# Two transformer blocks on one core: block 2's scores as two fp32r products on high and low halves, entry and end reordered

## The reference

```
def windowed_gqa(q, k, v, sink):
    qb = (q * (HEAD_DIM ** -0.5)).reshape(B, nb, BLOCK, N_KV_HEADS, Q_GROUP, HEAD_DIM)
    kb = band_blocks(k.reshape(B, S, N_KV_HEADS, HEAD_DIM), nb)
    ...
    scores = jnp.einsum("bnqhgd,bnkhd->bnhgqk", qb, kb).astype(jnp.float32)
    ...
    scores = scores - slopes * absdist.astype(jnp.float32)
    ...
    m = jnp.maximum(jnp.max(scores, axis=-1, keepdims=True), sink_l)
    p = jnp.exp(scores - m)
    denom = jnp.sum(p, axis=-1, keepdims=True) + jnp.exp(sink_l - m)
    p = (p / denom).astype(v.dtype)
    out = jnp.einsum("bnhgqk,bnkhd->bnqhgd", p, vb)
```

## Time and profile before

| what | value |
|---|---|
| time, median of 3 runs | 690.18 us (689.23 to 691.2) |
| the profiled execution's own time | 689.03 us |
| its span, first to last instruction | 687.2 us |
| TensorE busy, share of the span | 640.4 us, 93% |
| VectorE busy | 351.2 us, 51% |
| ScalarE busy | 290.0 us, 42% |
| GpSimd busy | 51.7 us, 8% |
| chain that ended last: TensorE, transfers, VectorE, ScalarE | 76%, 11%, 6%, 4% |

### The profile page before, as it was taken

How to read it: one execution, slowest core, us unless ns; L and a number is a source line. 1 busy time by engine, 2 the same in 40 slices (tenths; PEclk the granted TensorE clock), 3 DMA queues, 4 the chain that set the end, 5 groups by cost and what they waited for, 6 DMA issues and landing times.

```text
span 687.2 us, 10211 instructions
## 1 busy us (share of the span) xinstructions
PE 640.4 (93%) x4037; PEld 483.7 (70%) x4037; DVE 351.2 (51%) x678; ACT 290.0 (42%) x552; POOL 51.7 (8%) x76
## 2 busy tenths in 40 slices
PE   8999899999999776879899999999999999999995
PEld 5979888842543320424399999998788888888884
DVE  4687664731031020110187766657856666666665
ACT  5855562421011010100182755563665555544554
POOL 3100101100010000000049000000000000000001
PEclk9999999999999997799999999999999999999999
DMA  8956338999999999999997333345535555554101
GB/s 344 419 194 260 116 138 331 403 372 426 427 374 425 420 422 421 422 420 421 422 421 280 123 124 123 123 167 187 185 137 188 189 195 202 198 193 184 62 1 61
DMA packets 26286, 180.73 MB, mean 263 GB/s; under 512 B 3184, under 2 KB 3312, under 8 KB 5120
## 3 DMA queue, kind: packets, MB, share of 16 engines
q1 hardware_dynamic: 25488, 177.89, 65.4%
q10 hardware_dynamic: 752, 2.21, 0.8%
HBM read 179.04 MB, written 1.05 MB: 262 GB/s over the span
## 4 chain that ended last, share of the span: by engine, by line
PE 76%; DMA 11%; DVE 6%; ACT 4%; issue 2%; POOLq 0%; SPq 0%; POOL 0%; ACTq 0%; DVEq 0%
PE ps L1567 73%; DMA ring<-stream_dram 11%; PE ps L1570 3%; DVE ring_r L406 1%; ACT single L399 1%; DVE work L1502 1%; ACT work L850 1%; DVE work L1505 1%; ACT work L757 0%; DVE h L1555 0%; ACT turned L855 0%; ACT work_r L846 0%; DVE work L1388 0%; DVE single L1399 0%; ACT work L764 0%
## 5 line engine op out<-in xcount | busy, mean ns | idle before, releaser
L1567 PE MATMUL ps<-turned,single 128*128 128x256 f32 (+2 forms) x944 | 231.1, 326 | 1.6 <-ACT work L627 0.8
L1567 PE MATMUL ps<-turned,ring_r 128*128 128x256 f32 (+1 forms) x648 | 179.9, 281 | 0.0
L1567 PEld LDWEIGHTS ps<-turned,single 128*128 128x128 f32 x944 | 156.3, 189 | 18.4 <-issue 2.0
L406 DVE TENSOR_TENSOR ring_r<-ring,single 128x1024 fp32r<-128x1024 f32 (+1 forms) x132 | 160.8, 1240 | 14.7 <-ACT single L399 14.7
L399 ACT ACTIVATE single<-ring 128x1024 fp32r<-128x1024 f32 (+1 forms) x132 | 133.8, 1047 | 0.0
L1567 PEld LDWEIGHTS ps<-turned,ring_r 128*128 128x128 f32 x648 | 121.2, 189 | 0.4
L1567 PE MATMUL ps<-ring,work 128*32 128x512 f32 (+2 forms) x462 | 69.8, 612 | 14.7 <-DMA ring<-stream_dram 12.6
L1567 PEld LDWEIGHTS ps<-single 128*128 128x128 f32 x257 | 40.7, 199 | 34.8 <-issue 22.4
L1567 PE MATMUL ps<-work 128*128 128x128 f32 (+5 forms) x310 | 60.5, 378 | 2.6 <-DVE work L1046 1.8
L1567 PE MATMUL ps<-single,turned 128*128 128x512 f32 (+3 forms) x208 | 59.7, 367 | 1.9 <-DVE turned L1187 1.5
L1567 PE MATMUL ps<-single 128*128 128x512 f32 (+1 forms) x257 | 58.0, 367 | 2.9 <-DVE single L1399 1.9
(11 more groups left out here) (254 smaller groups left out, 697.4 us busy)
## 6 DMA issues: line engine op xcount, KB each, us to landing
ring<-stream_dram SPq DMA_DIRECT2D x145, 1024.0 KB, 12.0
work<-stream_dram SPq DMA_DIRECT2D x12, 1024.0 KB, 12.3
turned_w<-stream_dram SPq DMA_DIRECT2D x4, 1024.0 KB, 14.1
extra<-stream_dram SPq DMA_DIRECT2D x2, 1024.0 KB, 9.4
ring<-stream_dram SPq DMA_DIRECT2D x2, 832.0 KB, 7.2
h<-x_dram SPq DMA_DIRECT2D x2, 512.0 KB, 4.5
gain<-gains_dram ACTq DMA_DIRECT2D x2, 512.0 KB, 8.5
yields<-stream_dram SPq DMA_DIRECT2D x1, 1024.0 KB, 12.5
```

The costliest lines, as they stand in the source:

```text
L406: dve.tensor_tensor(ring_r[:, place, a], ring[:, place, a], w_hi[k % HIGHS][:, a].bitcast(F32), ALU.subtract).then_inc(s["wlo_done"], 1)
L1567: return pe.matmul(o, lhsT, rhs, start=start, stop=stop, **kw)
```

## The change

Block 2's scores: `q2_split` and `k2_split` are laid over `extra`, whose tiles have been read by then. For each query head `q2_split` holds the high half in the head's own 64 rows and the low half in the other 64 rows. For each key head `k2_split` holds the high half of K in both halves of the rows, and, for each place of the query head, the low half in 64 rows and zeros elsewhere (GpSimd clears these instead of `k2T`). The first product of a unit then gives high x high and low x high at once, the second high x low. ScalarE makes the high halves (`q2_high`, `k2_high`) between its weight splits, VectorE the low ones (`q2_low`, `k2_low`), three pairs ahead of the loop and three inside it, in units 3, 4 and 6. The two turns of K on TensorE and ScalarE's copies of them are gone.

The entry: TensorE, and with it the first transposes, waits for `cst`, `meta` and the first half of `h` alone; `vec` is issued by ScalarE as its second load; three idle products stand instead of four, and two instead of four later. The end: the last squares stand ahead of the second result; ScalarE itself issues the store of the third piece; SP's last store waits only for its own piece.

```
+        q2_split = halved(extra_r[:, 0, :], HEADS, TOK)
+        k2_split = halved(extra_r[:, 1, :], 6, TOK)
...
+        def q2_high(act, c):
+            act.wait_ge(s["q2_sb"], c + 1)
+            for hd in (2 * c, 2 * c + 1):
+                rows = q2_rows(hd, 0)
+                last = act.activation(q2_split[rows, hd, :], q2T[rows, c, :], ACT.Copy)
+            last.then_inc(s["qk_high"], 1)
...
+        def q2_low(dve, c):
+            dve.wait_ge(s["qk_high"], c + 1)
...
+                last = dve.tensor_tensor(q2_split[q2_rows(hd, 1), hd, :], q2T[rows, c, :], q2_split[rows, hd, :].bitcast(F32),
+                                         ALU.subtract)
...
+        def k2_low(dve, kv):
+            dve.wait_ge(s["zpad_done"], 3)
+            dve.wait_ge(s["qk_high"], CT + 2 * kv + 1)
...
-            sp.dma_start(vec[:, 0:V_RB], small[:, 0:V_RB]).then_inc(const_in, 16)
...
             act.dma_start(meta_raw, meta).then_inc(x_in, 16)
+            act.dma_start(vec[:, 0:V_RB], small[:, 0:V_RB]).then_inc(const_in, 16)
             act.dma_start(pos_i[:], positions).then_inc(const_in, 16)
...
             result(0, 0)
+            last_squares(1, 1)
             result(0, 1)
-            last_squares(1, 1)
             result(1, 0)
+            act.wait_ge(s["y_done"], NT + 1)
+            act.dma_start(out[P:TOK, 0:512], xn2[:, 1, column_half(0)]).then_inc(out_st, 16)
...
-            idle_products(ps[:, 7, 0:ZA], zt[:, 0, 0:P], zt[:, 0, :], 4)
-            pe.wait_ge(const_in, 48)
-            pe.wait_ge(x_in, 32)
+            idle_products(ps[:, 7, 0:ZA], zt[:, 0, 0:P], zt[:, 0, :], 3)
+            pe.wait_ge(x_in, 48)
...
-            idle_products(ps[:, 0, 0:ZA], zt[:, 0, 0:P], zt[:, 0, :], 4)
+            idle_products(ps[:, 0, 0:ZA], zt[:, 0, 0:P], zt[:, 0, :], 2)
...
-            mm(ps[0:HD, 1, 0:TOK], ident[:, HD:P], k2T[:, 3, :], True, True)
-            mm(ps[HD:P, 1, 0:TOK], ident[:, 0:HD], k2T[:, 0, :], True, True).then_inc(s["k2_ps"], 1)
...
             def scores2(u):
                 hd, i = u // 2, u % 2
-                if u == 2:
-                    pe.wait_ge(s["k2_sb"], 2)
+                kv = hd // 4
+                if u % 8 == 0:
+                    pe.wait_ge(s["qk_high"], CT + 2 * kv + 2)
+                    pe.wait_ge(s["qk_low"], 5 if kv else 3)
+                elif u == 12:
+                    pe.wait_ge(s["qk_low"], CT + 2)
                 if u >= 2:
                     pe.wait_ge(s["nm2_done"], u - 1)
-                mm(ps[:, 2 + u % 2, 0:TOK], q2T[:, hd // 2, i * P:(i + 1) * P], k2T[:, 2 * (hd // 4) + hd % 2, :],
-                   True, True).then_inc(s["s2_ps"], 1)
+                q = q2_split[:, hd, i * P:(i + 1) * P]
+                mm(ps[:, 2 + u % 2, 0:TOK], q, k2_split[:, kv, :], True, False)
+                mm(ps[:, 2 + u % 2, 0:TOK], q, k2_split[:, 2 + 2 * kv + hd % 2, :], False, True).then_inc(s["s2_ps"], 1)
```

More of the change, by code:

```diff
@@ L311, in two_blocks @@
         full = [sem(f"slot_full{i}") for i in range(SLOTS)]
-        extra_full = [sem(f"extra_full{i}") for i in range(EXTRA)]
         full2 = [sem(f"slot2_full{i}") for i in range(SLOTS)]
@@ L468, in attention2_low, with q2_rows, k2_high @@
                               ).then_inc(s["o2_low"], 1)
+        def q2_rows(hd, low):
+            return slice(HD, P) if hd % 2 != low else slice(0, HD)
+        def q2_high(act, c):
[6 more added lines that the diff above has]
+            dve.wait_ge(s["qk_high"], c + 1)
+            for hd in (2 * c, 2 * c + 1):
+                rows = q2_rows(hd, 0)
+                last = dve.tensor_tensor(q2_split[q2_rows(hd, 1), hd, :], q2T[rows, c, :], q2_split[rows, hd, :].bitcast(F32),
+                                         ALU.subtract)
+            last.then_inc(s["qk_low"], 1)
+        def k2_high(act, kv):
+            act.wait_ge(s["q2_sb"], CT + 1)
+            rows = slice(kv * HD, (kv + 1) * HD)
+            for other in (kv, 1 - kv):
+                act.activation(k2_split[other * HD:(other + 1) * HD, kv, :], k2T[rows, :], ACT.Copy).then_inc(s["qk_high"], 1)
+        def k2_low(dve, kv):
+            dve.wait_ge(s["zpad_done"], 3)
+            dve.wait_ge(s["qk_high"], CT + 2 * kv + 1)
+            rows = slice(kv * HD, (kv + 1) * HD)
+            for odd in (kv, 1 - kv):
+                to = slice(odd * HD, (odd + 1) * HD)
+                last = dve.tensor_tensor(k2_split[to, 2 + 2 * kv + odd, :], k2T[rows, :], k2_split[rows, kv, :].bitcast(F32),
+                                         ALU.subtract)
+            last.then_inc(s["qk_low"], 1)
         def gate_out(dve, m):
@@ L570, in _ @@
                              ).then_inc(full2[n % SLOTS], 16)
-            for i in range(NT):
-                for n in range(2):
-                    sp.wait_ge(s["y_done"], n + 1 if i == 0 else 2 * NT)
-                    sp.dma_start(out[i * P:(i + 1) * P, n * 512:(n + 1) * 512], xn2[:, i, n * 512:(n + 1) * 512]
-                                 ).then_inc(out_st, 16)
+            for n in range(2):
+                sp.wait_ge(s["y_done"], n + 1)
+                sp.dma_start(out[0:P, n * 512:(n + 1) * 512], xn2[:, 0, n * 512:(n + 1) * 512]).then_inc(out_st, 16)
+            sp.wait_ge(s["y_left"], 1)
+            sp.dma_start(out[P:TOK, 512:D], xn2[:, 1, 512:D]).then_inc(out_st, 16)
             sp.wait_ge(out_st, 16 * 2 * NT)
@@ L805, in _ @@
             split_high(act, SPLIT1 + 3)
+            q2_high(act, 0)
             split_high(act, SPLIT1 + 4)
+            q2_high(act, 1)
+            q2_high(act, 2)
             split_high(act, SPLIT1 + 5)
-            act.wait_ge(s["zpad_done"], 3)
-            act.wait_ge(s["k2_ps"], 2)
-            for c in range(2):
-                rows = slice((1 - c) * HD, (2 - c) * HD)
-                last = act.activation(k2T[rows, c + 1, :], ps[rows, 1, 0:TOK], ACT.Copy)
-            last.then_inc(s["k2_sb"], 1)
+            q2_high(act, 3)
+            k2_high(act, 0)
+            k2_high(act, 1)
             def values_out():
@@ L1454, in _ @@
                     split_low(dve, SPLIT1 + 3 + c // 2)
+                else:
+                    q2_low(dve, c // 2)
             dve.wait_ge(s["k2_ps"], 1)
-            dve.wait_ge(s["zpad_done"], 3)
-            for c in range(2):
-                rows = slice(c * HD, (c + 1) * HD)
-                last = dve.tensor_tensor(k2T[rows, 3 * c, :], ps[rows, 0, 0:TOK], row2[rows, :], ALU.mult)
-            last.then_inc(s["k2_sb"], 1)
+            dve.tensor_tensor(k2T, ps[:, 0, 0:TOK], row2, ALU.mult).then_inc(s["q2_sb"], 1)
+            k2_low(dve, 0)
             split_low(dve, SPLIT1 + 5)
```

36 lines of the change are left out of this document (21 added, 15 removed).

## The result

The changed kernel takes 683.67 us (median of 4 runs, 683.35 to 684.21) against 689.7 (688.82 to 691.2): a ratio of 0.9911, with a 95% interval of 0.9898 to 0.9925. The runs of before are the three that stood ahead of the prediction, with a median of 690.18, and one more of 688.82. The forecast was 684.6. The profiled execution took 683.71 us with a span of 681.9, 5.3 less than the span of before.

What follows compares the result with a forecast made beforehand. TensorE was taken to carry 76% of the chain of waits. Entry 1.65, block 2 3.0 and end 0.9 sum to 5.55 us: 684.6 us from the median 690.18, 683.5 from the profiled execution; range 682.4 to 687.0.

Steps and rivals of the forecast that it cites:

- The entry (1.65): Start of the kernel: earlier transposes and fewer idle products were to gain 1.65 us, bounds 0.9 and 2.0.
- So it does not wait: Entry: sixteen transposes lie ahead of the one needing `h`'s second half, due at 6.84 us, so no wait there.
- TensorE gets to its higher clock as early as before: Entry: condition under which the removed idle products cost nothing else, TensorE working without a pause up to there.
- rival *slower: Entry: TensorE pauses for a late load, clock stays at 1.2 GHz into the first products; 692 us and more; chance 0.04.
- Passing the expert stage: Expert stage, between entry and block 2: its beginning and end move with TensorE, so the whole 1.65 us passes.
- My rival in which the stage swallows the entry: Expert stage: if transfers set its start, the entry's 1.65 us is lost; 686.2 us; chance 0.13.
- Block 2's start (0.7): First scores of block 2: 0.88 us cheaper on TensorE, of which 0.7 counts, with a wait at the second turn.
- the first rival: Block 2's start: K's two low subtractions each wait behind a GpSimd operation; start worth 0.2, time 685.1 us; chance 0.17.
- The loop (2.3): Block 2's loop: two cheaper score products per unit, 12 units left at 0.19 us each, 2.3 us.
- the margin of 0.3: Block 2's loop, two units: with a pair VectorE needs 3.7 us to the next softmax row; TensorE comes after 4.0.
- the third rival: Block 2's loop: VectorE bounds it, or the new pair is not cheaper; loop gives 0.3, time 686.6 us; chance 0.12.
- The end (0.9): Last row: squares one scaling earlier, 0.47 us, and last store from ScalarE, 0.43; 0.9 taken, bounds 0.47 and 0.95.

## Why the prediction was right, step by step

- **The entry (1.65).** Right in size: 1.43 in the two profiles, 1.6 in the mean of the traces. Two steps failed singly. "So it does not wait" for `h`'s second half: it did in that execution, because a landing of 5.2 us is one of 4.8 to 6.1; TensorE also came for it earlier than forecast, with the transposes starting at 5.69 us and not 6.2. And that TensorE gets to its higher clock as early as before: in two executions of six it did not, and their marks are some 1.6 us behind the mean of the other four (14.15). That is the lower clock of my rival *slower*, but without the pause that the rival names, and I had given it 15 us of work at half rate. The rows show that it ended with the transposes or within the next idle product; so it takes most of the entry's gain in such an execution, and no more.
- **Passing the expert stage.** Right: whole, with -0.8 to +1.2 us on top, in which no run shows a gain or a loss by the change. Without +0.66 of that the profiled pair would differ by 4.7 and not 5.3. My rival in which the stage swallows the entry falls: at 150 us the shift was 1.47, at 342 us 2.09.
- **Block 2's start (0.7).** 0.67 and a wait at the second turn, as forecast, but by two errors that cancel. K's low pair took 1.73 us where I had put 0.85 + 0.4, since GpSimd stood beside both halves: the mechanism of the first rival, with the wait at the first score that I had named as a sign of being wrong. In turn GpSimd was done before the weight split behind it, which took 2.36 us and not the 3.02 of the earlier trace rows, and it ended when I had said. The rival's price, 0.5 of the start, was therefore not paid; without GpSimd the start is 0.46 better.
- **The loop (2.3).** Mechanism right, size off: 1.95. The units are 3.76 us (3.77 forecast), so the new pair is as much cheaper as the gate chunk's products said. The term mis-sized is the margin of 0.3: from the gate chunk's end (394.57) to the turn (398.52) VectorE and ScalarE needed 3.95 us, where I had 3.7, and TensorE came after 3.79, where I had 4.0. A margin of -0.16, in each of the two units: a part of the third rival (VectorE bounds the loop), 0.4 us of the 2.0 that I had given it. Moving the pairs gave it back (0.41).
- **The end (0.9).** 0.64. The squares gave their 0.47 (0.45 at the last scaling). The term mis-sized is the store: 0.43 forecast, about 0.2 measured, since the issue came 0.37 sooner but that store landed 2.4 us after it, and not 2.2. On SP the end is worth the same, so ScalarE's queue gained nothing; what helped was that SP's stores no longer wait for all the pieces (the last one issued 0.89 us behind the start of the last scaling, 1.12 before).
- **The sum.** 5.55 forecast; 5.3 in the profiles, 6.0 in the medians. The median fell 0.9 us below the forecast. Half of that is the base: the median of before was 690.18 with three runs and is 689.7 with four. The other half is 6.0 against 5.55, and it is not explained. The parts as traced (entry 1.6 to 2.0, block 2 2.62, end 0.64) add up to 4.9 to 5.3, and the changed kernel, run again beside the kernel before, gave 6.0 once more (683.59 against 689.55). The 0.7 to 1.1 us left are within what single executions differ by, but no trace shows what they are. That the forecast came this near is in part luck: the start held two errors that cancel, and the loop and the store were 0.6 us too high together.

## What to carry to other kernels

Price an edit of a tenth of a per cent by the shift of one instruction across the place, and the rest of the program by several executions: here one trace's landing of a load and one stage's clock were each worth as much as a part of the change. Two operations added to an engine off the chain need a margin counted to the end of the whole relay (gate output, pair, split, mask, exponential, scaling), not just their own duration. Where a new VectorE operation with two inputs in SBUF is on the path, look which GpSimd operation stands beside it and hold that one back if nobody waits for it.

## What the runs showed of the hardware that I had not expected

- The point at which TensorE reaches its higher clock in the first microseconds differs between executions of one program: the six half-products ahead of the transposes took 3.80 to 4.53 us, and in two of six executions the sixteen transposes behind them still took 3.6 to 3.7 us instead of 2.0 to 2.3. The granted clock read 1.00 in either case. Without idle products the sixteen took 3.67 us, and the first products of weights, behind a pause of 1.3 us, ran at the higher clock.
- From 310 to 330 us the granted clock was 0.91 in all three traces with the entry of before and 0.97 to 1.00 in the ten with a changed one, although the kernel with the entry alone has no edit near that place.
- The same load, issued at 1.64 us, landed 4.8 to 6.1 us later, whichever queue the small load beside it was on.
- A VectorE subtraction of 64 x 256 took 0.43 us alone and 0.87 beside GpSimd, whose own operations were not longer; beside a weight split of 128 x 1024, in the kernel before, one of these took 1.59 us instead of 0.76.
